# Scores inside the query projection, 176 dense tokens in layer 1, every twelfth output tile in plain fp32, in a two-layer hybrid trunk with product-key experts

## The reference

```python
q = (tb @ wq).reshape(PEER_BLOCK, PEER_HEADS, 2, PEER_HALF)      # 8 heads, 2 halves of 128
s = jnp.einsum('thpd,hpnd->thpn', q, keys)                       # 128 keys a half
sv, si = lax.top_k(s, PEER_TOPK)                                 # first level, 16 of 128
comb = sv[:, :, 0, :, None] + sv[:, :, 1, None, :]               # 16 x 16
fv, fi = lax.top_k(comb.reshape(...), PEER_TOPK)                 # second level
gate = jax.nn.softmax(fv, axis=-1)
hid = jax.nn.gelu(jnp.einsum('td,thkd->thk', tb, jnp.take(u_tab, eidx, axis=0)))
return jnp.einsum('thk,thkd->td', (gate * hid), jnp.take(v_tab, eidx, axis=0))
```

## Time and profile before

| | |
|---|---|
| median of 3 runs | 1913.82 us (1911.51 to 1914.9) |
| the profiled execution, its time | 1917.62 us |
| its span, first to last instruction | 1915.8 us |
| mean granted clock | 0.972 |
| PE / DVE / ACT / POOL busy | 97% / 74% / 46% / 41% |
| DMA | 472 MB, mean 246 GB/s |

### The profile page before, as it was taken

How to read it: one execution, slowest core, us unless ns; L and a number is a source line. 1 busy time by engine, 2 the same in 40 slices (tenths; PEclk the granted TensorE clock), 3 DMA queues, 4 the chain that set the end, 5 groups by cost and what they waited for, 6 DMA issues and landing times.

```text
span 1915.8 us, 39041 instructions
## 1 busy us (share of the span) xinstructions
PE 1853.9 (97%) x14352; PEld 1816.6 (95%) x14352; DVE 1414.6 (74%) x2834; ACT 890.1 (46%) x1861; POOL 794.0 (41%) x571
## 2 busy tenths in 40 slices
PE   9978899999999999999999879999999999999999
PEld 8966899999999999999989769999999999999998
DVE  2686409794599899999946763389717887889987
ACT  5523532111566755555555234312126666555554
POOL 4894550022243446665348946302401122334331
PEclk9977999999999999999999779999999999999999
DMA  5300355699799799999933004569987785999995
GB/s 194 128 2 1 110 176 176 203 375 353 262 344 343 281 330 385 378 373 381 356 115 131 2 1 142 174 202 347 364 308 251 258 294 182 341 348 349 349 349 197
DMA packets 129427, 472.18 MB, mean 246 GB/s; under 512 B 14368, under 2 KB 14496, under 8 KB 129056
## 3 DMA queue, kind: packets, MB, share of 16 engines
q1 hardware_dynamic: 87840, 319.66, 46.6%
q0 software_dynamic: 41472, 151.01, 21.3%
HBM read 469.56 MB, written 1.05 MB: 246 GB/s over the span
## 4 chain that ended last, share of the span: by engine, by line
PE 91%; DVE 7%; ACT 1%; issue 1%; DMA 0%; POOL 0%; SPq 0%; POOLq 0%; ACTq 0%; DVEq 0%
PE ps L1054 90%; DVE x L1581 1%; DVE arena L1596 0%; DVE x_lo L1574 0%; DVE arena L1626 0%; DMA w<-v_c 0%; DVE onehots_j L1569 0%; PE ps L1142 0%; DVE arena L1632 0%; DVE arena L1646 0%; DVE arena L1633 0%; DVE arena L1604 0%; DVE arena L1660 0%; DVE arena L1635 0%; DVE h L2063 0%
## 5 line engine op out<-in xcount | busy, mean ns | idle before, releaser
L1054 PE MATMUL ps<-x_hi,w_hi 128*128 128x384 f32 (+2 forms) x2720 | 788.3, 346 | 16.7 <-DVE x_lo L1574 11.4
L1054 PE MATMUL ps<-x_hi,w_lo 128*128 128x192 f32 (+2 forms) x2720 | 709.1, 261 | 0.0
L1054 PE MATMUL ps<-x,w 128*128 128x192 f32 x4096 | 682.4, 326 | 0.0
L1054 PEld LDWEIGHTS ps<-x,w 128*128 128x128 f32 x4096 | 663.4, 190 | 0.3 <-issue 0.3
L1054 PEld LDWEIGHTS ps<-x_hi,w_hi 128*128 128x128 f32 x2720 | 514.0, 189 | 24.0 <-DVE arena L1821 7.4
L1054 PEld LDWEIGHTS ps<-x_hi,w_lo 128*128 128x128 f32 x2720 | 521.5, 192 | 0.0
L751 ACT CAST w_hi<-w 128x1024 fp32r<-128x1024 f32 x340 | 357.3, 1051 | 285.0 <-DMA w<-v_c 220.4
L682 POOL DMA_INDIRECT arena<-v_c,sel x144 | 268.3, 1863 | 279.3 <-DVE arena L2044 256.0
L2030 DVE TENSOR_TENSOR w_lo<-w,w_hi 128x1024 fp32r<-128x1024 f32 x250 | 304.8, 1219 | 45.5 <-ACT w_hi L751 44.9
L651 POOL TENSOR_TENSOR w_lo<-w,w_hi 128x1024 fp32r<-128x1024 f32 x90 | 221.4, 2475 | 230.2 <-ACT w_hi L751 230.2
L682 POOL DMA_INDIRECT rows_w<-ur_c,sel x96 | 98.0, 1021 | 319.0 <-DVE sel L1854 229.4
(11 more groups left out here) (195 smaller groups left out, 1668.9 us busy)
## 6 DMA issues: line engine op xcount, KB each, us to landing
w<-u_c SPq DMA_DIRECT2D x256, 512.0 KB, 4.5
w<-v_c SPq DMA_DIRECT2D x256, 512.0 KB, 5.9
w<-w_c SPq DMA_DIRECT2D x84, 512.0 KB, 3.4
arena<-v_c,sel POOLq DMA_INDIRECT x144, 8.2
arena<-keys_c SPq DMA_DIRECT2D x2, 1024.0 KB, 6.7
arena<-mix_c SPq DMA_DIRECT2D x2, 964.0 KB, 8.5
rows_w<-ur_c,sel POOLq DMA_INDIRECT x96, 6.8
h<-h SPq DMA_DIRECT2D x2, 544.0 KB, 4.6
```

The source lines that it names most:

```text
L1054: return nc.tensor.matmul(out_, lhsT, rhs, start=start, stop=stop, skip_group_check=True)
```

## The change

- Scores and transposes are issued between the query tiles: the transposes of a group after query tiles 3, 7 and so on, the scores of head group g for the first and last token tile after query tiles 4, 8 and 12, the rest at the end. The keys are loaded earlier on SP's queue. DVE takes the first levels as they come (`first_level`), restores x after the fifth of them, and interleaves dots by a running cost count. The last request moves to `quiet + 2`, that is tile 56 and 52.
- Layer 1 has 176 dense tokens and 44 steps; 16 more tokens (`C_GROUP`) are gathered, so it has 80 slots in two groups. It has 7 row buffers for `v`, layer 0 still 5.
- Output tiles 5, 17, 29 and so on (11 in each layer) are plain fp32 matmuls on raw weights and raw hidden values: no high or low halves for them.
- The gates' one-hots are four `tensor_scalar` of 128 elements from SBUF in place of two operations of 512 through PSUM.

```diff
-ND = 192
+A_GROUP, C_GROUP, B_GROUP = (T - 64, 64), (T - 80, 16), (0, NMETA)
+DENSE = (192, 176)
+GROUPS = ((A_GROUP, B_GROUP), (A_GROUP, C_GROUP))
+SCORE_LAG = 4
+KEYS_AT = NZ + NOUT + NL + 1
+PLAIN_AT = 5
+NPLAIN = len(range(PLAIN_AT, NKEYS, UN))
+COST_FIRST, COST_SECOND, COST_WIDE, COST_SMALL, COST_DOT = 265, 410, 2290, 300, 1300
+SOFTMAX_AT, INDEX_AT, DOTS_AT = 4500, 12000, 21000
+PACE = (3300, 3600)
+DOTS_ASK = 3
+DOTS_REST = (17, 21)
+DOTS_END = (38, 38)
...
-        self.ask = self.split - 3
-        self.quiet = self.ask - 4
+        self.quiet = (54, 50)[l]
+        self.ask = self.quiet + 2
+        self.vrows = ARENA // D - P * self.nd // D - len(self.groups)
-        self.quiet_first = 22 if self.last else 30
+        self.quiet_first = {(192, 1): 25, (176, 1): 27, (192, 0): 18, (176, 0): 19}[self.nd, 1 - l]
...
+        def plain(i):
+            return i % UN == PLAIN_AT
...
-                times(sp, NL, NPROJ, lambda n, it: load(l, n, w_c[l, UN * it + n], it))
+                times(sp, NL, KEYS_AT, lambda n, it: load(l, n, w_c[l, UN * it + n], it))
                 sp.wait_ge(s_xn, (2 * l + 2) * DC)
                 sp.dma_start(keys.rearrange("p m n -> p (m n)"), keys_c[l]).then_inc(s_keys, 16)
+                times(sp, KEYS_AT, NPROJ, lambda n, it: load(l, n, w_c[l, UN * it + n], it))
...
+                for m in range(NQ):
+                    n = NZ + NOUT + m
+                    if m >= 2:
+                        pe.wait_ge(s_ea, l * (NZ + NQ) + NZ + m - 1)
+                    project(l, n, L.t0, ready=None if m else x_split(l, 2))
+                    x = m // 4
+                    if m % 4 == 3 and x < len(L.groups):
+                        pe.wait_ge(s_xd, X0[l] + x + 1)
+                        for c in range(DC):
+                            last = mm(ps[:, X_BANKS[x][c // 4], c % 4 * P:(c % 4 + 1) * P],
+                                      xs_rep[x][:, c * P:(c + 1) * P], ident, True, True)
+                        last.then_inc(s_xr, 1)
+                    if m >= SCORE_LAG and m % 4 == SCORE_LAG % 4:
+                        scores(L.scores[2 * (m - SCORE_LAG) // 4:2 * (m - SCORE_LAG) // 4 + 2])
+                scores(L.scores[6:])
...
-                        last = mm(ps[:, 1 + i % UB, 0:ND], wraw[:, g % NL, c, :], xn[:, c, E0:TG], c == 0, c == DC - 1)
+                        last = mm(ps[:, 1 + i % UB, 0:L.nd], wraw[:, g % NL, c, :], xn[:, c, E0:L.tg], c == 0, c == DC - 1)
...
-                mm(ps[:, IOTA_BANK, 0:P], ident, iota, True, True)
+                    if group == C_GROUP:
+                        r = slice(32, 64)
+                        for q in range(PACK):
+                            for x in range(2):
+                                e = 32 * q + 16 * x
+                                last = mm(o(slice(32 * q, 32 * (q + 1))), shift_up[r, 16 - 16 * x:48 - 16 * x],
+                                          chosen[r, 0, :, e:e + 16], x == 0, x == 1)
...
-                def chunk(i, c):
+                def chunk(i, c, it=0):
                     g = l * NW + NV0 + i
+                    if plain(i):
+                        return mm(ps[:, c, 0:L.nd], wraw[:, g % NL, c, :],
+                                  hid[l][:, bass.ds(UN * it + i, 1), :].squeeze(1), False, True)
...
+                for s, g in ((0, 0), (lastt, 0), (0, 1), (lastt, 1), (0, 2)):
+                    run(first_level(s, g))
+                restore()
+                run(first_level(0, 3))
+                run(second_level(0))
...
-                    v.tensor_tensor(eq, iota_ps, bc(sel[:, 1, g:g + OHT], 2, P), ALU.is_equal).then_inc(s_dl, 1)
-                    v.tensor_tensor(ohA[:, k % 2], eq, bc(sel[:, 0, g:g + OHT], 2, P), ALU.mult).then_inc(s_oh, 1)
+                    for t in range(OHT):
+                        g = OHT * k + t
+                        ins = v.tensor_scalar(ohA[:, k % 2, t, :], iota, sel[:, 1, g:g + 1], sel[:, 0, g:g + 1],
+                                              ALU.is_equal, ALU.mult)
+                    ins.then_inc(s_oh, 1)
...
+                gates(0)
+                for _ in range(DOTS_REST[l]):
+                    expert_dot()
```

More of the change, by code:

```diff
@@ L336, in trunk, with v_landed @@
         ident, ones, iota, shift = res("ident"), res("ones"), res("iota"), res("shift")
-        folds = [res(f"fold{g}") for g in range(len(GROUPS))]
+        shift_up, folds = res("shift_up"), {n: res(f"fold{n}") for n in (16, 64)}
+        def v_landed(l, m):
+            L = LAYERS[l]
+            b = m % L.vrows
+            before = sum(len(range(b, M.slots, M.vrows)) for M in LAYERS[:l] if b < M.vrows)
+            return b, before + m // L.vrows + 1
         def vcol(l, name, i=0, parts=slice(0, P)):
@@ L958, in _, with scores @@
                 x_high(l, 2, xn, L.t0)
+                def scores(pairs):
+                    for s, g in pairs:
+                        k = SC_OF[l][s, g] - 1
+                        act.wait_ge(s_qr, SC0[l] + k + 1)
+                        nc.scalar.copy(sc[:, s, 4 * g:4 * g + 4, :].rearrange("p m n -> p (m n)"),
+                                       ps[:, 5 + k % 2, :]).then_inc(s_sc, 1)
                 for m in range(NQ):
@@ L1454, in _ @@
                 asked()
[L1455 removed]
+                n = L.nd - P
                 for m in range(3):
[L1457 to L1461 removed]
@@ new lines, in _, with first_level @@
+                lastt = len(L.tiles) - 1
+                tops = lambda s: (topv[s == lastt], topi_u[s == lastt])
+                def first_level(s, g):
+                    dve.wait_ge(s_sc, SC0[l] + SC_OF[l][s, g])
+                    tv, ti_ = tops(s)
+                    yield from top16([(hh, p) for hh in (2 * g, 2 * g + 1) for p in range(2)],
+                                     lambda hh, p: tv[:, hh, p, :], lambda hh, p: ti_[:, hh, p, :],
+                                     lambda hh, p: sc[:, s, 2 * hh + p, :], COST_FIRST)
@@ L2006, in apply @@
                     ins.then_inc(s_gm, 1)
-                matches(0)
                 gates(0)
+                for _ in range(DOTS_REST[l]):
+                    expert_dot()
+                left, end = L.slots - dots[0], DOTS_END[l]
                 for k in range(L.steps):
                     if k + 1 < L.steps:
-                        matches(k + 1)
-                    for n in L.dots_step[k]:
-                        expert_dot(n)
+                        gates(k + 1)
+                    for _ in range(left * min(k + 1, end) // end - left * min(k, end) // end):
+                        expert_dot()
                     tile_gates(k)
-                    if k + 1 < L.steps:
-                        gates(k + 1)
                     apply(k)
                 def act_low(i):
-                    dve.wait_ge(s_ah, l * NKEYS + i + 1)
+                    if plain(i):
+                        return
+                    dve.wait_ge(s_ah, l * (NKEYS - NPLAIN) + v_split(i) + 1)
                     ah, al_ = act_pair(L, i)
```

353 lines of the change are left out of this document (183 added, 170 removed).

## The result

The changed kernel takes **1881.8 us** (median of 4 runs, 1876.75 to 1883.34) against 1913.82: a ratio of .983, 95% interval .9814 to .9845. The forecast was 1881. The profiled execution took 1882.99 us, its span 1881.2, so 34.6 us less than the 1915.8 of before.

What follows compares the result with a forecast made beforehand. PE (TensorE) was taken to bound the kernel, chain for 91% of the span. Terms from -27.3 us (layer 1 hidden records) to +3.4 (plain tiles) summed to -32.7 us: 1881 us by the median, range 1872 to 1897.

Steps and rivals of the forecast that it cites:

- Hidden tiles and steps of layer 1: Layer 1: shorter matmul records -27.3 us, 44 instead of 48 steps -3.6, added small matmuls +1.0, iota matmul gone.
- Output pair: Layer 1 output tiles: first matmul saves 13.3 ns, second nothing because its weight load is not covered; -12.5 us.
- Rival 1: Output tiles: weight loads do not bound the second matmul, 6.2 us more saved, about 1875 us; chance .12.
- DMA term: Layer 1's output stage: weights and rows need 394 GB/s; taken as +2 us, of 0 to +9.
- rival 2: Layer 1's output stage: DMA is the bound, sustaining only 381 GB/s; 1888 us, up to 1893; chance .18.
- Plain tiles: Output stages, 11 plain tiles a layer: +3.4 us in layer 0, +1.0 in layer 1, relieving DVE.
- Projection: Query projections: moved scores and transposes cost 0; a second group's transposing matmuls add 1.95 us in layer 1.
- Selection: Starts some 30 us sooner, in the projection; last request at tile 56 and 52, 33 us slack in layer 0; cost 0.
- Rival 5: Selection comes late at tile 56 or 52, PE waits 5 to 20 us a layer; 1890 to 1915 us; chance .05.
- Rival 3: Projection: DVE's searches and GpSimd's subtractions contend, low halves 3.3 us, PE waits 9 us; 1890 us; chance .05.
- Gates: Steps: four tensor_scalar take 1.0 us of DVE, hidden behind PE; at upper bounds +17 us in all.
- rival 4: Steps: the gates' tensor_scalar wait for GpSimd's gather issues, +88 us, 1969 us; chance .04.

Runs made afterwards that it cites:

- e4: The changed kernel with 192 dense tokens in both layers and one gathered group in layer 1: 1923.41 us, ratio 1.0027 to the kernel before.
- e6: The changed kernel with the second matmul of every output pair streaming 48 more columns: 1884.07 us, ratio .9833 to the kernel before.
- e5: The changed kernel run and profiled again with no edit: 1883.04 us, ratio .9839 to the kernel before.
- e12: The changed kernel once more with no edit, a single execution: 1889.87 us.
- e1: The changed kernel, but layer 1's gathers fetch half of each value row and the sum reads it twice: 1881.7 us, ratio .9805 to the kernel before.
- e2: The changed kernel, but in layer 1 DVE sums only half of each fully fetched value row: 1882.05 us, ratio .981 to the kernel before.
- e7: The changed kernel with scores and transposes behind the query tiles again and x restored before the first levels: 1912.69 us, ratio .9995 to the kernel before.
- e3: The changed kernel with no plain output tiles in either layer: 1877.57 us, ratio .9803 to the kernel before.
- e9: The changed kernel with 176 dense tokens in both layers, 30 instead of 17 layer 0 dots before the steps, plain tiles only in layer 0: 1852.82 us.
- e10: The changed kernel with no dots between the last request and the steps: 1909.33 us, ratio .9973 to the kernel before.
- e8: The changed kernel with 176 dense tokens and a third gathered group in layer 0 too: 1863.48 us, ratio .9736 to the kernel before.
- e11: The changed kernel with five instead of seven value row buffers in layer 1: 1887.86 us, ratio .9853 to the kernel before.

## Why the prediction was right, and where it was not

The large terms were right, and the errors of the small ones, up to 4 us each, went both ways. That the median fell within 1 us of the forecast is partly luck.

- **Hidden tiles and steps of layer 1.** Forecast -27.3 - 3.6 + 1.0 - .2 = -30.1, measured -30.6 in three profiles. A record was 149 ns (2.39/16) and a step 3.28 as worked out. e4 shows that without the 176 tokens there is none of it.
- **Output pair.** Forecast 273 ns with a second matmul that gains nothing, measured 2.19 us for eight. e6 shows what was only inferred, that the second stream does not set the pair: 48 more columns there cost .9 ns and nothing. That it is the weight load which does was not varied by itself. The Trainium skill (TensorE: Matmul & The Clock Gate, LDWEIGHTS) has a load of 128 columns take 107 ns; e6 agrees in that a second stream of up to 240 columns, 100 ns at 2.4 GHz, is free. Rival 1 is out.
- **DMA term.** This step was mis-sized, and differently for each execution. +2 was taken of 0 to +9. In the first profile after, output tiles 1 changed by -4.0 instead of -7.75, so with the other terms as forecast it was +5.8 there. In e5 and e12 they changed by -8.1 and -7.6 with a fall of the clock in them that the prediction did not have, by -9.7 and -9.1 without: the term was 0 and .6. The chain of waits of the first profile after, in order of time, shows where its loss arises:

```profile
1605.73 8.72 DMA w<-v_c
...
1614.55 1.06 ACT w_hi L785
...
1615.90 0.87 issue
1616.78 0.33 DVE x_hi L2122
1617.11 1.20 DVE arena L2146
```

  A weight tile lands 8.7 us after its issue (median 6.2), the cast follows, and DVE, which works in order, has a row sum before the next low half. There are five such places, with landings after 7.4 to 8.7 us; PE is 70% of the chain from 1580 us to the end and the `v` weights 13.5%, where e5 has PE for 96%. By its own sign ("wrong if PE is no longer the chain in layer 1's output stage") the prediction was at its edge in this one execution. What made the tiles late is open: half the bytes (e1), half the sums (e2) and no edit at all (e5, e12, e7) leave out the loss alike. It is not a rate that the memory can't give; rival 2's ground ("381 GB/s being all it sustains") is refuted by 391 to 401 GB/s over 100 us with PE full (e5, e12, e2, e3, e9).
- **Plain tiles.** Forecast +3.4 in layer 0. Measured 3.0 to 3.1 (e3). The stage itself grew by only 1.3 to 1.5, because the kernel before had lost some 1.6 us to the clock near its end, 3.4 us at 1.2 GHz:

```profile
960.00:970.00 10.00, 8.67 (x55) 8.44 (x53) 6.01 (x21) 1.71 (x3) 3.84 (x3) 0.83 0.25 68
```

  In layer 1 the claim "without the plain tiles ... no cover at all" was too strong: 128 x 1.40 + 80 x 1.20 = 275 us of DVE stand against 128 x 2.19 = 280 of PE. At these 98% e3 gave back the 2.2 us that it should have saved, and e9 kept 2.0 of them.
- **Projection.** Forecast 0 and +1.95, measured +.4 to +.8 and +2.3. The difference is a .47 us wait of the last scores for ScalarE's copy. That the move costs nothing was nearly right; e7 shows what it buys.
- **Selection.** The 33 us of slack were computed for the last request. PE waits at neither last request, and behind it DVE waits 28.5 us for the first step in layer 0 and 30.6 in layer 1, so it was there. What the prediction did not work out is the first request, at tile 27 and 21 instead of 32 and 24: without the early scores it comes 11.1 and 15.3 us late (e7). Rival 5 is out.
- **Rival 3.** GpSimd took 32.50/13 = 2.5 us for a low half in layer 0's projection beside DVE's first levels, as before, and the same in layer 1's. It is out.
- **Gates, rival 4.** Four tensor_scalar were put at 1.0 us, bounds .6 to 1.44. (The +17 us at the upper bound is a slip: .2 x 38 + .3 x 38 is 19.) DVE in order of time, and the line's minimum, median and maximum in ns:

```profile
1504.26 1.12 DVE L2078 TENSOR_SCALAR onehots_i<-res,sel 128x128 f32<-128x128 f32 x4
1505.29 1.22 DVE L1929 CUSTOM_DVE_ANT_0 rows_x<-rows_x,arena 128x1024 f32<-128x1024 f32 x1
```

```profile
L2078 DVE TENSOR_SCALAR onehots_i<-res,sel x368: 329/343/2312, 435.6 to 1578.6; 128x128 f32<-128x128 f32 x184
```

  They issue in 1.03 us. Rival 4 is out: GpSimd issues a gather in those steps and the median stays 343 ns. e10 shows how thin the cover of the steps is: half a dot more a step and DVE sets it.
- **Unforeseen and small:** the two mixers, which no edit touches, gave 3.2 + .8 us of the 34.6 by chance; that made up for the DMA term of that execution. Falls of the clock near the end of the output tiles move a stage by 1.6 us.

## What to carry to other kernels

Where one matmul of a pair streams fewer columns than a weight load takes, cut columns from the other one, and price them one by one. A gain of columns on TensorE is only as large as VectorE's work per step allows, so move VectorE's work into the gap ahead of the steps in the same edit: that was worth 10 us here (362.4 to 352.1). Compare stages and not totals when an untouched stage ahead swings by 10 us. Look at the granted clock inside each stage too, and profile the unedited kernel again before a few microseconds are put down to an edit: here a second profile without any edit took as much off the stage as two experiments that were made to explain it.

## What the hardware showed that I had not expected

- A GpSimd subtraction held a DVE tensor_scalar for its whole length, while gathers issued on GpSimd did not. The last steps of layer 1, GpSimd and DVE in order of time:

```profile
1572.46 2.36 POOL L683 TENSOR_TENSOR w_lo<-w,w_hi 128x1024 fp32r<-128x1024 f32 x1 [15.06 <-ACT w_hi L785]
1575.74 2.37 POOL L683 TENSOR_TENSOR w_lo<-w,w_hi 128x1024 fp32r<-128x1024 f32 x1 [0.92 <-ACT w_hi L785]
```

```profile
1572.61 3.06 DVE L2078 TENSOR_SCALAR onehots_i<-res,sel 128x128 f32<-128x128 f32 x4
1576.49 2.46 DVE L2078 TENSOR_SCALAR onehots_i<-res,sel 128x128 f32<-128x128 f32 x4
```

  Four take 3.06 and 2.46 us instead of 1.12; the line's longest single one is 2312 ns. Beside the four of 1504.26 above, GpSimd issued this gather:

```profile
1503.81 0.94 POOL L715 DMA_INDIRECT rows_x<-ur_c,sel  x1 [1.12 <-DVE sel L1929]
```

  The Trainium skill (SBUF — State Buffer, "SBUF: two separate sides") has the two engines share a port pair as an exclusive lock. The trace agrees for GpSimd's arithmetic at these two places, and not for its gathers: the one shown takes .94 us, the four beside it 1.12, and the median of the tensor_scalars stays 343 ns.
- The granted clock of the first mixer, in the same stretch of the same code, was .88, .87 and .79 in three profiles, and the projection began at 223.8, 226.6 and 234.5 us.
- Layer 1's hidden part took 348.39 us in every profile of the changed kernel and in e6 and e8, but 350.4 to 350.7 in e1, e2, e3 and e9 and 349.2 in e11, whose edits don't touch it, with .3 to 1.3 us of "issue" idle in front of matmuls. The longer ones all ran on two of the chips, so that chip and program can't be told apart. The cause is open.
